# A two-layer transformer kernel on one core: ScalarE rounds each dense weight tile two units ahead of TensorE instead of one, VectorE's subtraction stays one unit ahead

## What is computed

```python
p = h @ w_in[l]                                   # first block, IN_COLS columns
x = x + y @ w_out[l]
h = h + _even_mixer(...)                          # h @ ev_w_in, ..., @ ev_w_out
h = h + _cross(_rms(h, xa_norm[i]), _rms(mem, xa_mem_norm[i]), xa_wq[i], xa_wkv[i], xa_wo[i])
h = h + _mlp(_rms(h, mlp_norm[i]), mlp_w1[i], mlp_w2[i])   # square(relu(h @ w1)) @ w2
```

## Time and profile before

| | |
|---|---|
| time, median of 3 | 2228.4 us |
| time of the profiled execution | 2233.36 us |
| its span in the profile | 2232.1 us |
| TensorE busy | 2058.3 us (92%), 11400 matmuls |
| VectorE busy | 1139.0 us (51%) |
| ScalarE busy | 868.8 us (39%) |
| subtractions (line 171) | 293, mean 1223 ns |
| roundings (line 165) | 293, mean 1052 ns |

### The profile page before, as it was taken

The page is one execution under the profiler, slowest core; times in us unless marked ns, Lnnn a source line. Parts: engine busy times, 40 slices in busy tenths (PEclk is TensorE's granted clock), DMA queues, the critical chain, the costliest instruction groups (busy, mean ns, idle before and its releaser), DMA issues.

```text
span 2232.1 us, 28369 instructions
## 1 busy us (share of the span) xinstructions
PE 2058.3 (92%) x11400; PEld 1628.2 (73%) x11400; DVE 1139.0 (51%) x2014; ACT 868.8 (39%) x1567; POOL 18.9 (1%) x68
## 2 busy tenths in 40 slices
PE   6898878898979999999999999999989999999997
PEld 4665656777756577878888888676667878888886
DVE  5566568736466455445343345344445445343444
ACT  4324443245243443344232233465644344232332
POOL 0000000000000000000000000000000000000000
PEclk8889889999979899999999999999999999999999
DMA  5210011013201023312322323111122322322322
GB/s 195 77 57 20 20 38 48 2 55 120 85 29 66 1 85 104 100 61 95 104 95 95 104 90 99 57 48 57 38 73 97 104 67 95 104 94 95 100 90 75
DMA packets 52052, 169.64 MB, mean 76 GB/s; under 512 B 5777, under 2 KB 9425, under 8 KB 51921
## 3 DMA queue, kind: packets, MB, share of 16 engines
q1 hardware_dynamic: 51920, 167.82, 23.0%
HBM read 165.70 MB, written 2.10 MB: 75 GB/s over the span
## 4 chain that ended last, share of the span: by engine, by line
PE 59%; DVE 4%; ACT 3%; issue 1%; POOL 0%; DVEq 0%; ACTq 0%
PE ps L152 58%; DVE wr L171 1%; PE ps L157 1%; ACT wr L165 1%; DVE st L403 1%; DVE x_pr L390 0%; DVE macc L233 0%; ACT x_pr L421 0%; DVE X L1522 0%; ACT x_pt L432 0%; ACT sa_sp L2102 0%; DVE st L406 0%; ACT msq L226 0%; ACT sa_sp L2100 0%; ACT sb_sp L2105 0%
## 5 line engine op out<-in xcount | busy, mean ns | idle before, releaser
L152 PE MATMUL ps<-hi,wr 128*128 128x512 f32 (+1 forms) x4616 | 1410.6, 385 | 58.2 <-DVE wr L171 41.4
L152 PEld LDWEIGHTS ps<-hi,wr 128*128 128x128 f32 x4616 | 863.2, 190 | 239.8 <-DVE wr L171 24.9
L152 PE MATMUL ps<-lo,wr 128*128 128x512 f32 (+1 forms) x2308 | 880.5, 381 | 0.0
L152 PEld LDWEIGHTS ps<-lo,wr 128*128 128x128 f32 x2308 | 440.2, 191 | 84.5 <-issue 3.9
L171 DVE TENSOR_TENSOR wr<-raw,wr 128x1024 fp32r<-128x1024 f32 x293 | 358.3, 1223 | 145.4 <-ACT wr L165 145.2
L165 ACT ACTIVATE wr<-raw 128x1024 fp32r<-128x1024 f32 x293 | 304.7, 1052 | 236.5 <-PE ps L152 236.5
L1449 DVE TENSOR_TENSOR X<-X,ps 128x512 f32<-128x512 f32 x96 | 66.0, 687 | 226.3 <-PE ps L152 226.3
L1985 ACT ACTIVATE mlp<-mlp 128x512 f32<-128x512 f32 x64 | 40.4, 632 | 241.4 <-DVE mlp L1968 241.4
L1968 DVE SCALAR_TENSOR_TENSOR mlp<-ps,R 128x512 f32<-128x512 f32 x64 | 44.3, 691 | 94.6 <-PE ps L152 87.4
L1971 DVE TENSOR_TENSOR lo<-mlp,hi 128x512 fp32r<-128x512 f32 x64 | 44.3, 692 | 87.5 <-ACT hi L1989 87.5
L213 ACT ACTIVATE hi<-X,pv 128x512 fp32r<-128x512 f32 x48 | 34.6, 722 | 136.4 <-DVE X L1449 134.6
(11 more groups left out here) (694 smaller groups left out, 1921.5 us busy)
## 6 DMA issues: line engine op xcount, KB each, us to landing
raw<-d_w SPq DMA_DIRECT2D x128, 512.0 KB, 3.5
raw<-d_wkv SPq DMA_DIRECT2D x32, 512.0 KB, 3.5
raw<-d_w_in SPq DMA_DIRECT2D x30, 512.0 KB, 3.5
raw<-d_sb_w_in SPq DMA_DIRECT2D x24, 512.0 KB, 3.4
raw<-d_ev_w_in SPq DMA_DIRECT2D x16, 512.0 KB, 3.4
raw<-d_wq SPq DMA_DIRECT2D x16, 512.0 KB, 3.4
raw<-d_wo SPq DMA_DIRECT2D x16, 512.0 KB, 3.5
X<-d_xT SPq DMA_DIRECT2D x16, 256.0 KB, 5.2
```

The source lines that it names most:

```text
L152: return pe.matmul(out, lhsT, rhs, start=start, stop=stop, skip_group_check=True)
```

## The change

ScalarE's `weight_hi` rounds unit n+2 in the step of unit n, where it rounded n+1. To get ahead, `start_scalar` rounds unit 1 behind the last of its activation tiles. VectorE's `weight_lo` is not touched. SyncE's wait and its eight loads of `xT` stand behind the load of the third `w_out` unit and not of the first.

```diff
 def weight_hi(K, M, a):
 
-    u = K.next_unit("act") + 1
+    u = K.next_unit("act") + 2
     if u < len(K.units):
         round_unit(K, M, a, u)
...
         if i == 1:
             round_unit(K, M, a, 0)
         square(K, a, N0, i, M.X[i], g.x_acc, g.x_tmp)
+    round_unit(K, M, a, 1)
...
-        if (name, u) == ("w_out", 0):
+        if (name, u) == ("w_out", 2):
             s.wait_ge(*K.done("pe", "rw", 1, "var"))
             for i in range(ND):
                 load(K, s, f"x{i}", M.X[i], dram["xT"][i])
```

## The result

| | before | after |
|---|---|---|
| median | 2229.49 us (4 runs, 2228.18 to 2231.14) | 2204.73 us (4 runs, 2203.17 to 2210.41) |
| profiled execution | 2233.36 us, span 2232.1 | 2210.41 us, span 2209.1 |
| ratio of the times | | 0.9895, 95% interval 0.9869 to 0.9922 |

The changed kernel is faster by 23.4 us by the ratio (17.4 to 29.2). The forecast was 2210.9 us, a gain of 17.5.

A forecast was written before the change was run, and what follows sets the result against it. TensorE, busy 92% of the span, was taken as the bound, so only its idle time could yield gains. Terms from 1.4 at unit 2 to -0.3 summed to 17.5 us, taking 2228.4 to 2210.9 us; range 2203 to 2220.

The forecast's parts named there:

- Units 2, 4, 24, 25, 29, the mixer: Places where VectorE idles for roundings: gains 1.4, 4.2, 1.8 (24 and 25 together), 1.0; first mixer 2.5 and 1.3 us.
- The wait for `db_pr`: First mixer, behind unit 53's subtraction: TensorE's wait of 3.29 us nearly all goes, gain 2.5 us.
- A sign that the prediction gave for being wrong: Over the profile after: TensorE's idle time is the same and only names another releaser.
- The clock at units 24 and 25: Unit 24 at full clock; unit 25, behind a 3.9 us wait, loses 1.5 to 2.5 us; net gain 1.8.
- The cross attentions ... I take 2.4 us per layer: Both cross attentions: four TensorE waits each, 2.60 us in all, caused by late roundings; 4.8 us gained together.
- The charge of 0.3 us at unit 62: Unit 62's rounding waits for unit 59's end, so ScalarE's copy comes 0.3 us later; counted as -0.3 us.
- SyncE's part at nothing: SyncE's moved xT loads, needed by unit 34's residual after RWKV's third and fourth pair: no cost.
- The wait of about 31 us for line 171: TensorE's total waits for VectorE's subtraction, line 171, expected to fall from 44.6 to about 31 us.
- The smaller gain: Rival: second-hand gains at db_pr, x_pr, units 23 and 24 do not carry; 10.5 us gain, 2217.9 us; chance 0.20.
- The bigger gain by the clock: Rival: full clock gives up to 2.4 us more at unit 4, 2.1 at 25; 22.0 us, 2206.4; chance 0.15.
- No change: Rival: VectorE's freed time lies ahead of evacuations waiting for TensorE; under 4.5 us, 2226 us; chance 0.06.
- Slower by the hold: Rival: in-order ScalarE, held by early roundings, delays head exponentials 0.3 us each, 23 us; 2234 us; chance 0.06.

The follow-up runs named there:

- e3_xt_only: The kernel before with SyncE's part of the change alone, roundings one ahead as before: 2232.21 us, ratio 1.0015.
- e2_rest: The kernel before with ScalarE rounding two ahead only from unit 42 to the end, SyncE's loads as before: 2214.46 us, ratio 0.993.
- e1_first_block: The changed kernel with ScalarE rounding two ahead only up to unit 41, one ahead behind it: 2222.13 us, ratio 0.9951.
- e9_after_again: The changed kernel itself measured once more, nothing altered: 2208.62 us, ratio 0.9906.
- e6_three_ahead: The changed kernel with ScalarE rounding three units ahead among the heads of cross and stick-breaking attention, 57 steps: 2212.81 us.
- e4_unit4_late: The changed kernel with unit 4's rounding put back behind the RWKV chain, together with unit 5's: 2213.25 us, one run.
- e10_early_lo5: The changed kernel with VectorE's subtraction moved ahead of long chains in eleven places, and unit 5 rounded right behind unit 4: 2181.39 us, ratio 0.9793.
- the fill: The kernel before with products of no use in TensorE's waits ahead of units 4, 24 and 72: 2228.11 us, ratio 0.9992.

## Why the prediction was right, and where its sum was off

Distances between first products, us. "One ahead" are profiles that have the old roundings there (before, e3_xt_only, e2_rest up to unit 41, e1_first_block behind it), "two ahead" the others (after, e9_after_again and the complement); given is the value on which they agree (but e3_xt_only took 16.5 at 21 to 23, at a higher clock). Where no values stand, the clock of units 72, 93 or 221 differs between the profiles, and the gain is that of pairs in which it did not: for 72 to 93 before and e9_after_again, 121.6 and 118.0; the profiled pair itself shows 4.7 there, 1.1 of it by unit 72's clock.

```
stretch                         one ahead  two ahead   gain  forecast
0 to 2     unit 2                   18.48      17.00    1.5       1.4
3 to 4     unit 4                   14.53      10.22    4.3       4.2
21 to 23                            17.1       16.7     0.4       0.3
23 to 26   units 24, 25             24.87      22.45    2.4       1.8
26 to 29   unit 29                  33.55      32.45    1.1       1.0
52 to 53   db_pr                    24.15      21.52    2.6       2.5
53 to 54                             4.69       3.17    1.5       1.3
54 to 60                            34.53      34.44    0.1
72 to 93   cross attention, first                       3.6       2.4
189 to 221 cross attention, second                      3.4       2.4
93 to 103, 221 to 231   MLPs                            0.7       0.5
```

The sum is 21.6 us; with the forecast's charge of 0.3 it was 17.5. The second measurement of the changed kernel gave 21.0 and the first 23.4. The profiled pair shows 23.0: the 21.6, and a balance of the clock's chances (2.7 at 188 to 189, 1.4 at units 4 and 5, 1.1 at unit 72, against 1.1 at unit 93, 1.0 at 20 to 21 and 0.9 at unit 7, among others).

- **Units 2, 4, 24, 25, 29, the mixer: right in size**, each within 0.6 us. VectorE's idle time was the limit of each gain, as the earlier trace rows had it (at unit 24 it was TensorE's own wait, 4.10 us), and unit 25's new wait is 3.84 us where 3.9 was forecast.
- **The wait for `db_pr`: the gain is right, its path is not.** The forecast had TensorE's wait of 3.29 us go and nothing in its place. It fell to 0.62, but two other waits grew behind it, and TensorE's idle time from unit 52 to 53 is 4.8 us as before. The waits of the changed kernel, and the windows of 52 to 53 in the kernel before, in the changed one and in e6_three_ahead:

```profile
637.95 0.52 PE L157 MATMUL ps<-cst,dc_pr 128*128 128x128 f32 x3 [1.75 <-DVE dc_pr L1603]
...
642.78 0.63 PE L157 MATMUL ps<-cst,db_pr 128*128 128x128 f32 x4 [2.26 <-DVE st L1597]
```

```profile
638.05:662.20 24.15, 19.37 (x88) 14.12 (x87) 18.02 (x39) 11.08 (x26) 0.00 (x0) 0.82 0.07 23
```

```profile
629.05:650.57 21.52, 16.74 (x88) 12.17 (x87) 19.06 (x41) 11.07 (x26) 0.00 (x0) 0.95 0.07 26
```

```profile
628.87:650.39 21.52, 18.36 (x88) 13.44 (x87) 19.07 (x41) 11.09 (x26) 0.00 (x0) 0.87 0.08 26
```

  The last two take the same time at different clocks of TensorE. What sets the first 18 us is VectorE, which in the changed kernel has no pause of over 0.2 us there; in the kernel before it had one, the 2.56 us of the earlier trace rows, and this is the gain. A sign that the prediction gave for being wrong, TensorE's idle time the same under other names, is met here although the time fell. (A slow stretch late in 52 to 53 does cost: e4_unit4_late and e10_early_lo5 took 23.1 us.)
- **The clock at units 24 and 25: right in the profile, with one reason missing.** Unit 24 ran at full clock and unit 25 at 0.77. But the 2.4 us that unit 24 lost in the kernel before had cost nothing, since VectorE was late next; the fill shows it. In the changed kernel unit 26's data is ready, so unit 25's slow stretch is paid: 1.6 us (7.32 for 5.69). The term was 3.9 less this stretch, taken at 2.1; with 1.6 it is 2.3, and it measured 2.4 where 1.8 was forecast.
- **"The cross attentions ... I take 2.4 us per layer": the term that was too small**, by 2.2 us for both. A layer gave 3.4 to 3.6. The four waits of 2.60 us gave 2.65 (74 to 75, 79 to 80, 82 to 83 and 84 to 85 together). The other 1.0 us of the first layer lies in nine distances that became 0.05 to 0.3 us shorter each. I had left them out, as hardly any has a wait that can be listed: a product's record lasts 0.39 us where the next one starts after 0.23, so a shorter delay opens no gap between them. TensorE's listed idle time from 73 to 93 fell by 2.75 us only, and the distance by 3.7.
- **The charge of 0.3 us at unit 62: the delay came, the cost did not.** The copy now stands directly behind the rounding:

```profile
688.44 1.06 ACT L165 ACTIVATE wr<-raw 128x1024 fp32r<-128x1024 f32 x1 [4.38 <-PE ps L152]
689.41 0.58 ACT L1802 ACTIVATE mla_kn<-ps 128x512 f32<-128x512 f32 x1
```

  It starts 6.66 us behind unit 59's first product, where it started 6.32 behind it (unit 59 starts at 682.75 now and started at 695.99), so 0.3 us later. TensorE's next wait for ScalarE is 0.83 us in both and ends 9.7 us behind unit 59's first product in both, so no product waited for it.
- **SyncE's part at nothing: no cost is seen** in e3_xt_only.
- **"... the mean granted clock lies between the two only in stretches that hold such a wait"** is too wide: the window from 147 to 166 above has a clock of 0.55 with no wait over 2.01 us, against the 3.44 and 4.10 us meant. The stretches without a term that moved, such as 12 to 17 and 60 to 61, are pieces of this kind.
- **The wait of about 31 us for line 171** was an error of addition: the items of the forecast themselves make 44.6 - 1.4 (unit 2) - 4.1 + 2.7 (24, 25) - 1.1 (29) - 1.4 (54) - 3.1 (six short ones), 36.2, and with 0.5 at the start and 0.8 at unit 5 the 37.5 of the profile.

The rivals. *The smaller gain* is out: each of its second-hand pieces is there, and 10.5 us lie outside the interval. *The bigger gain by the clock* describes the profiled execution at unit 4, and not the kernel: in e9_after_again unit 4 was slow again. The 2.1 us at unit 25 that it added did not come in any of the five profiles in which unit 25 waits 3.84 us. It is chance, and with it its 22 us; that the changed kernel comes near 22 has other reasons, the cross attentions above all. *No change* is out by the intervals. *Slower by the hold* is out by e6_three_ahead: a hold longer by 117 us moved the heads nowhere, and cost 0.6 us at one place ahead of each of two groups of heads. The reason on record, that the work behind the rounding needs a later product anyway, is what the shrinking waits for `x_pr` show.

## What to carry to other kernels

When a stage is done ahead, look at once for who is late next. Here it was VectorE, whose subtraction stood behind long chains; moving that in eleven places gave as much again as the change itself. Where TensorE is the limit, a wait costs its length, and here often 1.5 to 2.8 us more if it was followed by products whose data was ready; products of no use inside such a wait brought nine units back to full clock, which is a gain only if they end before the wait does and no other engine is late next. In a stretch that VectorE sets, as the one of `db_pr`, TensorE's idle time says nothing of the gain: look at the limiting engine's own pauses. And before a surplus of 2 or 3 us in one profile is explained, take the same stretch from a second profile of the same program.

## What was not expected of the hardware

- Units that had waited from 2.0 to 7.1 us mostly ran slow, but not always: unit 93 after 2.51 us took 7.1 to 8.4 us in eleven profiles and 5.71 in one (e6_three_ahead); unit 4 after about 3 us took 3.10, 4.34 and 5.46. Unit 61 after 2.02 us was slow in all of its twelve profiles without fill, unit 31 after 2.1 us in none of four. After 1.18 us unit 25 was at full clock, and after 1.47 unit 189 in all 14.
- In latent attention the clock stayed at half for 24 us while the records show TensorE busy without a pause.
- Stretches with the same instructions take one of a few values: 188 to 189 48.9 us or 51.3 to 51.8, and nothing between, in 14 profiles.
